# First-half gate products of the first three experts ahead of the second half of the first gather

## What is computed

```python
def hier_moe(x, w_grp, b_grp, w_exp_router, b_exp_router, w_gate, w_up, w_down):
    ...
    for gi in range(N_GROUPS):
        hid = jax.nn.silu(jnp.einsum('td,edf->tef', x, w_gate[gi])) * jnp.einsum('td,edf->tef', x, w_up[gi])
        y = y + jnp.einsum('tef,efd->td', hid * dense_w[:, gi, :, None], w_down[gi])
    return y
```

## Time and profile before

| what | value |
|---|---|
| median of 3 runs | 1142.33 us (1142.23 to 1142.94) |
| the profiled execution | 1144.86 us |
| its span, first to last instruction | 1143.0 us |
| TensorE busy | 998.4 us (87%) |
| VectorE, ScalarE, GpSimd busy | 355.7, 224.1, 87.2 us |
| DMA, mean over the span | 301 GB/s, 343.81 MB |
| mean granted clock of TensorE | 0.965 |

### The profile page before, as it was taken

The page is one execution under the profiler, slowest core; times in us unless marked ns, Lnnn a source line. Parts: engine busy times, 40 slices in busy tenths (PEclk is TensorE's granted clock), DMA queues, the critical chain, the costliest instruction groups (busy, mean ns, idle before and its releaser), DMA issues.

```text
span 1143.0 us, 16010 instructions
## 1 busy us (share of the span) xinstructions
PE 998.4 (87%) x6758; PEld 709.3 (62%) x6758; DVE 355.7 (31%) x655; ACT 224.1 (20%) x474; POOL 87.2 (8%) x109
## 2 busy tenths in 40 slices
PE   7999999999999999999999989976758776766665
PEld 6888888778877777778888656533334343433321
DVE  3303484358213224236311131221262111111113
ACT  2111214203422222244100032110101011110102
POOL 0001121010123222300000000000000000000000
PEclk9999999999999999999999999999988899899987
DMA  9974457494659888974444979999999999999992
GB/s 317 292 258 150 148 187 268 155 284 145 190 202 315 286 313 294 301 264 159 140 147 175 384 296 417 416 416 416 418 417 417 416 417 416 416 417 417 416 417 111
DMA packets 138473, 343.81 MB, mean 301 GB/s; under 512 B 7784, under 2 KB 90984, under 8 KB 122008
## 3 DMA queue, kind: packets, MB, share of 16 engines
q1 hardware_dynamic: 122752, 287.97, 67.0%
q0 software_dynamic: 14496, 52.68, 13.1%
q10 hardware_dynamic: 1152, 2.10, 0.5%
HBM read 320.50 MB, written 22.20 MB: 300 GB/s over the span
## 4 chain that ended last, share of the span: by engine, by line
PE 65%; SPq 15%; DMA 11%; DVE 6%; ACT 2%; issue 1%; DVEq 0%; ACTq 0%
PE psum L998 36%; SPq L830 15%; DMA arena<-in_w_up 10%; PE psum L715 4%; PE psum L698 3%; PE psum L1047 3%; PE psum L725 3%; PE psum L1007 2%; PE psum L1059 2%; PE psum L760 2%; PE psum L1203 1%; PE psum L1191 1%; DVE arena L1744 1%; ACT arena L1342 1%; PE psum L1182 1%
## 5 line engine op out<-in xcount | busy, mean ns | idle before, releaser
L998 PE MATMUL psum<-arena 128*128 128x264 f32 x2048 | 473.1, 387 | 0.7 <-DVE arena L1879 0.6
L998 PEld LDWEIGHTS psum<-arena 128*128 128x128 f32 x2048 | 385.0, 190 | 80.5 <-issue 17.8
L715 PE MATMUL psum<-arena 128*32 128x256 f32 x2048 | 140.7, 424 | 83.7 <-DMA arena<-in_w_up 83.0
L715 PEld LDWEIGHTS psum<-arena 128*32 128x32 f32 x2048 | 75.2, 119 | 141.5 <-issue 113.2
L1342 ACT ACTIVATE arena<-psum 128x264 f32<-128x264 f32 (+3 forms) x148 | 61.3, 427 | 317.0 <-PE psum L998 240.8
L725 PE MATMUL psum<-arena 128*32 128x256 f32 x1024 | 66.0, 400 | 10.9 <-ACT arena L1588 10.6
L1342 ACT ACTIVATE arena<-arena 128x1024 f32<-128x1024 f32 (+6 forms) x62 | 55.1, 918 | 99.5 <-DVE arena L1899 87.8
L698 PE MATMUL psum<-arena 128*128 128x128 f32 (+1 forms) x384 | 74.3, 322 | 0.1
L698 PEld LDWEIGHTS psum<-arena 128*128 128x128 f32 (+1 forms) x384 | 55.8, 200 | 27.6 <-issue 16.3
L1852 DVE SCALAR_TENSOR_TENSOR arena<-arena 128x512 f32<-128x512 f32 x64 | 43.8, 747 | 91.6 <-ACT arena L1342 91.5
L2048 DVE SCALAR_TENSOR_TENSOR arena<-arena,psum 128x128 f32<-128x128 f32 x32 | 9.2, 287 | 194.5 <-ACT arena L1572 194.5
(11 more groups left out here) (246 smaller groups left out, 723.6 us busy)
## 6 DMA issues: line engine op xcount, KB each, us to landing
arena<-in_w_gate SPq DMA_DIRECT2D x64, 1024.0 KB, 23.1
arena<-in_w_up SPq DMA_DIRECT2D x64, 1024.0 KB, 23.0
arena<-in_w_down SPq DMA_DIRECT2D x64, 1024.0 KB, 23.1
arena<-in_w_in SPq DMA_DIRECT2D x48, 1024.0 KB, 5.5
arena<-in_state_ret POOLq DMA_DIRECT2D x16, 1024.0 KB, 7.0
out_ret_s<-arena POOLq DMA_DIRECT2D x16, 1024.0 KB, 7.5
arena<-in_w_mem_kv SPq DMA_DIRECT2D x8, 1024.0 KB, 11.6
arena<-in_cache_mem_k POOLq DMA_DIRECT2D x8, 1024.0 KB, 5.7
```

Of the source, the lines that this page charges most:

```text
L715: mm = pe.matmul(psum[32 * a:32 * a + SLOTS, bank, 0:256], tokens[:, 4 * half + k, SLOTS * j:SLOTS * (j + 1)], w[:, :, k, P * a:P * (a + 1 ...
L998: mm = pe.matmul(ps(task)[:, 0:T], w[:, k, (i % 2) * P:(i % 2 + 1) * P], rhs[:, k, :], start=k == 0, stop=k == KT - 1 and not two)
```

## The change

On TensorE the first gate halves of experts 0, 1 and 2 run one after the other as soon as the first half of the first quad's tokens is there, before gather parts 2 and 3. For that they need three banks at once: expert 0 uses bank 0, expert 1 bank 1, expert 2 bank 3. The last row piece (k = 7) moves from bank 1 to bank 3, so that expert 1 need not wait for it, and expert 2's first gate half waits until that piece is taken. Since bank 3 now holds expert 2's half-done products, expert 0's down product moves from bank 3 to bank 4; expert 1's down product, in bank 4 too, now waits until expert 0's result has been copied out. ScalarE and VectorE read from the banks that the new functions name; their order, and the order of SyncE's loads, is as before. The code before the loop over experts, and the loop's head:

```diff
         def row_bank(k):
-            return (0, 1, 3)[k % 3]
+            return 3 if k == KT - 1 else (0, 1, 3)[k % 3]
...
             if k >= 3:
-                pe.wait_ge(row_taken, k - 2)
+                pe.wait_ge(row_taken, KT - 2 if k == KT - 1 else k - 2)
...
+        AHEAD = 3
+        def gate_bank(e):
+            return (0, 1, 3)[e] if e < AHEAD else e % 2
+        def down_bank(e):
+            return 3 + e % 2 if e else 4
...
             make_rows(pe, 7)
+            pe.wait_ge(tokens_ready, 1)
+            for e in range(AHEAD):
+                tile_loaded(pe, e, 0)
+                tile_loaded(pe, e, 1)
+                if gate_bank(e) == row_bank(KT - 1):
+                    pe.wait_ge(row_taken, KT)
+                gate_up(pe, e, 0, XgT[:, 0], tile_at(e, 0), gate_bank(e)).then_inc(gate_up_half, 1)
             for e in range(EXPERTS):
                 q, j = divmod(e, 4)
                 base = tile_at(e, 0)
-                if j == 0:
-                    pe.wait_ge(tokens_ready, 2 * q + 1)
                 if e >= 2:
                     pe.wait_ge(hid_ready, e - 1)
-                tile_loaded(pe, e, 0)
-                tile_loaded(pe, e, 1)
-                gate_up(pe, j, 0, XgT[:, q % 2], base, e % 2).then_inc(gate_up_half, 1)
+                if e >= AHEAD:
+                    if j == 0:
+                        pe.wait_ge(tokens_ready, 2 * q + 1)
+                    tile_loaded(pe, e, 0)
+                    tile_loaded(pe, e, 1)
+                    gate_up(pe, j, 0, XgT[:, q % 2], base, gate_bank(e)).then_inc(gate_up_half, 1)
...
-                gate_up(pe, j, 1, XgT[:, q % 2], base, e % 2).then_inc(gate_up_full, 1)
+                gate_up(pe, j, 1, XgT[:, q % 2], base, gate_bank(e)).then_inc(gate_up_full, 1)
...
-                if e >= 2:
-                    pe.wait_ge(y_low_ready, e - 1)
-                    pe.wait_ge(y_high_ready, e - 1)
+                if e:
+                    pe.wait_ge(y_low_ready, max(e - 1, 1))
+                    pe.wait_ge(y_high_ready, max(e - 1, 1))
                 tile_loaded(pe, e, 4)
-                down(pe, 0, hT[:, e % 2, :], base, 3 + e % 2).then_inc(down_half, 1)
+                down(pe, 0, hT[:, e % 2, :], base, down_bank(e)).then_inc(down_half, 1)
...
-                A.activation(tg, psum[:, e % 2, 0:P], ACT.Tanh, scale=0.5).then_inc(gate_tanh, 1)
+                A.activation(tg, psum[:, gate_bank(e), 0:P], ACT.Tanh, scale=0.5).then_inc(gate_tanh, 1)
```

More of the change, by code:

```diff
@@ L1286, in _ @@
                 pe.wait_ge(hidT_ready, e + 1)
-                if e >= 2:
-                    pe.wait_ge(y_low_ready, e - 1)
-                    pe.wait_ge(y_high_ready, e - 1)
+                if e:
+                    pe.wait_ge(y_low_ready, max(e - 1, 1))
+                    pe.wait_ge(y_high_ready, max(e - 1, 1))
                 tile_loaded(pe, e, 4)
-                down(pe, 0, hT[:, e % 2, :], base, 3 + e % 2).then_inc(down_half, 1)
+                down(pe, 0, hT[:, e % 2, :], base, down_bank(e)).then_inc(down_half, 1)
                 tile_loaded(pe, e, 5)
-                down(pe, 1, hT[:, e % 2, :], base, 3 + e % 2).then_inc(y_full, 1)
+                down(pe, 1, hT[:, e % 2, :], base, down_bank(e)).then_inc(y_full, 1)
             pe.wait_ge(y_low_ready, EXPERTS)
@@ L1594, in _ @@
                     act.wait_ge(scatter_full, 6 * (q - 1))
-                low_rows(q % 2, j, 3 + e % 2)
+                low_rows(q % 2, j, down_bank(e))
             act.wait_ge(routed, 1)
@@ L2047, in _ @@
                 dve.wait_ge(gate_tanh, e + 1)
-                V.scalar_tensor_tensor(tmid, tg, 1.0, psum[:, e % 2, 0:P], ALU.add, ALU.mult).then_inc(swish_mid, 1)
+                V.scalar_tensor_tensor(tmid, tg, 1.0, psum[:, gate_bank(e), 0:P], ALU.add, ALU.mult).then_inc(swish_mid, 1)
                 dve.wait_ge(swish_mid, e + 1)
                 dve.wait_ge(hidT_full, e)
-                V.tensor_tensor(hid, tmid, psum[:, e % 2, P:2 * P], ALU.mult).then_inc(hid_ready, 1)
+                V.tensor_tensor(hid, tmid, psum[:, gate_bank(e), P:2 * P], ALU.mult).then_inc(hid_ready, 1)
                 if e == 0:
@@ L2070, in _ @@
                     dve.wait_ge(scatter_full, 6 * (q - 1))
-                high_rows(q % 2, j, 3 + e % 2)
+                high_rows(q % 2, j, down_bank(e))
                 if e == 12:
```

## The result

The changed kernel takes 1146.18 us (median of 7 runs, 1145.98 to 1146.90) against 1142.33 us before: +3.85 us, a ratio of 1.0031 with a 95% interval of 1.0022 to 1.0041. The forecast was 1145.9. The kernel is slower by more than the 0.2% that can be told from no change.

A forecast was written before the change was run, and what follows sets the result against it. The prediction took the expert weights' DMA stream to bound the kernel, only its start being movable. Terms 3.56 + 0 + 0 + 0 = +3.56 us on the median 1142.33 gave 1145.9, range 1143.9 to 1147.6.

The forecast's parts named there:

- What bounds: Expert weights: DMA is full from 686 to 1116 us, so only the stream's start, with two holes, can gain or lose.
- The moved matmuls, 3.56 us: 64 matmuls of experts 1 and 2 before the gather delay expert 3's parts 2 and 3: +3.56 us.
- the last gate half 3.5 us later: Sign at the end of the weights: the last expert's last gate half starts 3.5 us later.
- What queues behind: SP's queue: the second hole grows by 3.56 us; expert 4's early-freed loads wait behind expert 3's, adding 0.
- Banks and waits, 0: Moved banks and added waits for the last row piece, expert 2's first half and expert 1's down product: 0.
- The clock, 1.50 on both sides: Expert 0's second gate half takes 3.36 us instead of 1.86; this 1.50 was counted before and after the change.
- 11.8 us between the loads: Sign in SP's queue: expert 3's parts 2 and 3 go out some 11.8 us after parts 0 and 1, instead of 8.25.
- The clock staying up (1): Rival: expert 0's second half runs at full clock, 1.9 us instead of 3.4; +2.06, time 1144.4; chance 0.13.
- More clock lost (3): Rival: low clock on the gather or the gate halves ahead of it, up to +5.2, 1147.5 us; chance 0.10.
- The early release filling the hole (4): Rival: expert 4's parts 0 and 1 load before expert 3's parts 2 and 3, saving 2.3 us, 1140.0; chance 0.03.
- Nothing at the end (5): Rival: the weight stream catches up over the experts, so the time stays 1142.3 us; chance 0.04.
- The tail (2): Rival: last gate half and scatter products run at full clock, giving back 2.7 us; +0.9, 1143.2 us; chance 0.06.

The follow-up runs named there:

- the fourth experiment: Changed kernel with SP's loads reordered, parts 0 and 1 of experts 3, 4 and 5 first: 1141.39 us, ratio 0.9981 against the kernel before.
- the second profile: Profile of the changed kernel run once more with no edit: 1146.18 us, ratio 1.0030 against the kernel before.
- the second experiment: Changed kernel with one expert ahead instead of three, keeping bank moves and added waits: 1142.54 us, ratio 0.9998 against the kernel before.
- The first four experiments: Kernel before unchanged, 1142.67 us; changed kernel with one expert ahead, 1142.54; with two ahead, 1143.13; with three ahead and loads reordered, 1141.39.
- the last four: Changed kernel again, 1146.18 us; its two moved halves behind the gather, 1144.88; behind expert 0's second half, 1145.25; two experts ahead with loads reordered, 1141.47.
- the fifth: Changed kernel run once more with no edit: 1146.18 us, ratio 1.0030 against the kernel before.
- seventh: Changed kernel with the first halves of experts 1 and 2 behind expert 0's second half: 1145.25 us, ratio 1.0019 against the kernel before.
- eighth: Changed kernel with two experts ahead and parts 0 and 1 of experts 3 and 4 loaded first: 1141.47 us, ratio 0.9986 against the kernel before.
- the sixth: Changed kernel with the first halves of experts 1 and 2 behind gather parts 2 and 3: 1144.88 us, ratio 1.0019 against the kernel before.

## Why the prediction was right

- *What bounds.* Right. In all ten profiles the rate is 416 or 417 GB/s over the 400 us behind the first 24, and the loss in those 24 goes with the result: at full clock 3.28 lost before, 3.34 with the banks alone, 5.01 with one half in front, 6.79 with two.
- *The moved matmuls, 3.56 us.* Right as a term: 3.46 in the chain, 3.51 in the stream, at either clock. The medians say 3.85 and 3.4. The sign that the prediction asked for at the end, the last gate half 3.5 us later, came a little short: 3.08 at full clock and 3.23 at the low one, counted from the first load. Single profiles don't settle which is closer.
- *What queues behind.* Right. Expert 4's parts, free early, went out behind part 5 of expert 3, and the fourth experiment shows that the order of the queue kept them from filling the hole. The time for part 0 of expert 4, about 691.2, is a slip in the sum: the rows give 686.70 + 3.56 + 1.24 = 691.50, and in the second profile it went out at 691.51. Nothing rests on it.
- *Banks and waits, 0.* Right by the second experiment, and for expert 2's wait by the run of 96.
- *The clock, 1.50 on both sides.* The difference came out, but the reason as I put it did not. I took the low clock for a trait of the place, since the same gather and the same wait stand in front of it in both orders. It does not go with the order: the kernel before had it in one of two profiles, the changed kernel in one of two as well. It cost the stream 1.38 us on each side (4.66 - 3.28 and 8.17 - 6.79), where I put 1.50, since the half takes 1.98 at full clock behind the wait and not 1.86. The medians show the whole difference if the runs without a profile have the low clock about as often in both kernels, which no run shows; to that extent it was luck that 1145.9 came within 0.3 us. What I looked for in the profile, 11.8 us between the loads, came only in the second one (11.62); the first had 10.29.
- *The rivals.* The clock staying up (1): its sign came in the first profile after (1.98 instead of 3.36), its time of 1144.4 did not. As a consequence of the change it falls, since the clock stays up or drops in both orders. More clock lost (3) falls: the gather took 4.23 or 4.24 us in both profiles before and both after, and the 96 gate matmuls 5.32 in both. The early release filling the hole (4) failed just where its condition was put, at the order of the queue. Nothing at the end (5) falls by the measured time. The tail (2) gave back 1.2 us in the first pair of profiles, but its clock wanders within one kernel too: the last gate half took 3.64 and 1.93 us in the two profiles of the kernel before, 2.44 and 3.26 in those of the changed kernel. Whether the change shifts how often the tail has the low clock, no run tells.

## What to carry to other kernels

Where a stage is fed by one in-order queue of loads, an early release is worth something only if its load stands next in that queue (6.79 against 1.44 us lost here); before computing ahead, look which semaphore the queue's head waits for, and compute that first. Work put in front of the product that the queue's head waits for delays the loads by its own time; if such work is moved forward, the order of the loads should be moved with it. Two profiles of the same kernel are needed before two kernels' profiles are subtracted.

## What was not expected of the hardware

The granted clock at one place of one kernel came out at either level: over expert 0's second half TensorE ran at 2.4 GHz (1.98 us) in one profile of the kernel before and fell to 1.2 GHz (3.36 us) in the other, with the same instructions before it; likewise 1.98 and 3.28 in the changed kernel. What the level goes with is open. For the first pair of profiles no chip is on record. The first four experiments ran on one chip and show 1.98 us there each time; the last four ran on another, and there the low clock stood at this place in the fifth (3.28), seventh (a run of 96 in 7.07 us) and eighth (3.54), but not in the sixth (96 in 5.36). So the chip is a rival to chance from execution to execution.

The Trainium skill (TensorE: Matmul & The Clock Gate, "What's actually happening") says that the gate's measuring runs freely and does not start anew with the kernel. The four profiles of the two kernels are in keeping with that; with the chip open, they don't show it. The same section of the Trainium skill has it that recent work lifts the clock, which was the ground of the first rival; with 96 gate matmuls ahead of the gather instead of 32, the clock still fell in one of two profiles.

The first load of the stage also wandered, from 675.39 to 676.85 in two profiles of the same kernel. With the clock and the tail, that makes a single profile good to about 2 us here (the spans of the two profiles of the kernel before are 1143.0 and 1141.2), where the stretch of 24 us gave the same 3.51 twice.
